# Attention scores of two heads at a time in a float32 two-layer kernel: rotary parts as neighbouring 64-row tiles, mask in fp32r, later turns, output tiles spread

## What is computed

```python
s = (jnp.einsum('bqhd,bkhd->bhqk', qn, k_nope)        # 128 values a head
     + jnp.einsum('bqhr,bkr->bhqk', qr, k_pe)) * sm_scale   # 64 rotary values, key shared by heads
s = jnp.where(q_idx[:, None] >= k_idx[None, :], s, -jnp.inf)
p = jax.nn.softmax(s, axis=-1)
o = jnp.einsum('bhqk,bkhd->bqhd', p, v)
...
y = jnp.concatenate([y_rnn, y_att * silu(ga)], axis=-1) @ w_out
```

## Time and profile before

| what | value |
|---|---|
| runs | 2192.72, 2194.42, 2194.52 us, median 2194.42 |
| profiled execution | 2192.71 us, span 2190.9 us |
| granted TensorE clock, mean | 0.992 |
| TensorE busy | 2144.7 us, 98% |
| VectorE busy | 1282.7 us, 59% |
| ScalarE busy | 780.2 us, 36% |

### The profile page before, as it was taken

The page is one execution under the profiler, slowest core; times in us unless marked ns, Lnnn a source line. Parts: engine busy times, 40 slices in busy tenths (PEclk is TensorE's granted clock), DMA queues, the critical chain, the costliest instruction groups (busy, mean ns, idle before and its releaser), DMA issues.

```text
span 2190.9 us, 27655 instructions
## 1 busy us (share of the span) xinstructions
PE 2144.7 (98%) x9998; PEld 1699.1 (78%) x9998; DVE 1282.7 (59%) x2112; ACT 780.2 (36%) x1023; POOL 88.9 (4%) x130
## 2 busy tenths in 40 slices
PE   7999999999999999999999999989999999999999
PEld 5887877778787778777788888768877778776787
DVE  5567767677777767678752323262237777566333
ACT  5232424323242423334441212352234446554211
POOL 0000000000000000000000000000000001100000
PEclk9999999999999999999999999999999999999999
DMA  6555556555555655555463423433332322012332
GB/s 214 168 152 164 175 153 177 151 146 168 167 164 158 177 151 164 159 156 181 157 226 106 154 96 132 143 103 105 96 88 67 101 75 87 34 58 67 126 115 96
DMA packets 213856, 294.44 MB, mean 134 GB/s; under 512 B 16074, under 2 KB 150114, under 8 KB 212642
## 3 DMA queue, kind: packets, MB, share of 16 engines
q1 hardware_dynamic: 200722, 256.12, 38.1%
q0 software_dynamic: 8624, 29.04, 4.8%
q10 hardware_dynamic: 4448, 8.45, 1.1%
HBM read 273.51 MB, written 20.05 MB: 134 GB/s over the span
## 4 chain that ended last, share of the span: by engine, by line
PE 95%; DVE 2%; ACT 1%; DMA 1%; issue 1%; ACTq 0%; POOL 0%; DVEq 0%; SPq 0%; POOLq 0%
PE ps L2220 28%; PE ps L2221 28%; PE ps L2222 28%; PE ps L2308 2%; PE ps L2312 1%; PE ps L2549 1%; PE ps L2547 1%; PE ps L2569 1%; PE ps L2460 1%; PE ps L2290 1%; PE ps L2550 1%; PE ps L2560 0%; PE ps L2385 0%; PE ps L2292 0%; DMA vrows<-in_kv_a_norm_dram 0%
## 5 line engine op out<-in xcount | busy, mean ns | idle before, releaser
L2220 PE MATMUL ps<-hn_hi,w_hi 128*128 128x512 f32 x1280 | 517.8, 405 | 0.1
L2221 PE MATMUL ps<-hn_lo,w_hi 128*128 128x512 f32 x1280 | 505.6, 395 | 0.0
L2222 PE MATMUL ps<-hn_hi,w_lo 128*128 128x512 f32 x1280 | 505.5, 395 | 0.0
L1658 DVE TENSOR_TENSOR w_lo<-w_raw,w_hi 128x1024 fp32r<-128x1024 f32 x174 | 213.4, 1229 | 426.6 <-ACT w_hi L1047 425.1
L1047 ACT ACTIVATE w_hi<-w_raw 128x1024 fp32r<-128x1024 f32 x174 | 183.8, 1060 | 486.7 <-PE ps L2222 446.3
L1407 DVE TENSOR_TENSOR w_lo<-w_raw,w_hi 128x1024 fp32r<-128x1024 f32 x162 | 198.2, 1224 | 227.7 <-ACT w_hi L920 227.2
L920 ACT ACTIVATE w_hi<-w_raw 128x1024 fp32r<-128x1024 f32 x162 | 171.3, 1058 | 432.3 <-PE ps L2222 413.4
L2220 PEld LDWEIGHTS ps<-hn_hi,w_hi 128*128 128x128 f32 x1280 | 240.1, 188 | 62.6 <-DVE w_lo L1407 3.4
L2221 PEld LDWEIGHTS ps<-hn_lo,w_hi 128*128 128x128 f32 x1280 | 240.2, 188 | 60.7 <-issue 5.0
L2222 PEld LDWEIGHTS ps<-hn_hi,w_lo 128*128 128x128 f32 x1280 | 239.9, 187 | 58.8
L2220 PE MATMUL ps<-w_hi,y_hi 128*128 128x512 f32 x512 | 205.7, 402 | 7.5 <-DVE y_lo L1667 7.5
(11 more groups left out here) (366 smaller groups left out, 2690.3 us busy)
## 6 DMA issues: line engine op xcount, KB each, us to landing
ada_raw<-in_w_ada_dram SPq DMA_DIRECT2D x128, 384.0 KB, 3.4
w_raw<-in_ssm_w_in_dram SPq DMA_DIRECT2D x96, 512.0 KB, 4.6
w_raw<-in_ssm_w_in_dram SPq DMA_DIRECT2D x128, 256.0 KB, 4.2
w_raw<-in_w_in_dram SPq DMA_DIRECT2D x64, 512.0 KB, 3.9
w_raw<-in_ssm_w_out_dram SPq DMA_DIRECT2D x60, 512.0 KB, 3.9
csb<-cs_rows POOLq DMA_DIRECT2D x32, 512.0 KB, 6.8
w_raw<-in_w_out_dram SPq DMA_DIRECT2D x32, 512.0 KB, 3.9
y_rows<-yt POOLq DMA_DIRECT2D x8, 1024.0 KB, 4.7
```

The lines of the kernel that those rows point to most:

```text
L1658: nc.vector.tensor_tensor(w_lo[:, slot, :], w_raw[:, slot, :], w_hi[:, slot, :].bitcast(F32), ALU.subtract).then_inc(lo_ready, 1)
L2220: nc.tensor.matmul(out_, a_hi, b_hi, start=start, stop=False)
L2221: nc.tensor.matmul(out_, a_hi, b_lo, start=False, stop=False)
L2222: return nc.tensor.matmul(out_, a_lo, b_hi, start=False, stop=stop)
```

## The change

A step k is now a query block and a head, `k % 2, k // 2`, so both heads of one block are neighbours. TensorE's `score(p, j)` makes both heads of block j: for each head the 128-row product and the mask, then the two rotary products one behind the other. Identity and mask are copied to fp32r once (`ident_r`, `mask_r`, by ScalarE), and the mask product uses them. The order of TensorE, VectorE and ScalarE within a pair is written anew. Some small buffers move into `ysq`.

```diff
+def head_and_rows(k):
+    return k % 2, k // 2
...
             def turned(g):
...
-                act.wait_ge(root_asked, g + 4)
-                nc.scalar.activation(nrm[:], nrm[:], ACT.Sqrt).then_inc(root_done, 1)
                 act.wait_ge(q_turned, g + 1)
                 for h, bank in enumerate(Q_BANKS):
...
                 if g + 1 < PAIRS:
                     read_tile(g + 1, 0)
+                act.wait_ge(root_asked, g + 4)
+                nc.scalar.activation(nrm[:], nrm[:], ACT.Sqrt).then_inc(root_done, 1)
+                if g + 1 < PAIRS:
                     read_tile(g + 1, 1)
...
                 for k in range(8):
-                    if cur and 1 <= k <= 5:
-                        read_tile(g, k + 2)
+                    if cur and k in (2, 4, 6):
+                        for t in range(k + 1, min(k + 3, 8)):
+                            read_tile(g, t)
+                    if cur and k == 6:
+                        pair_hi(g * 4 + 6)
...
-                        if g + 1 == PAIRS:
-                            make_y2_hi(k - 6)
+                    if g + 1 == PAIRS and k in (4, 5):
+                        make_y2_hi(k - 4)
...
+            act.wait_ge(mask_ready, 1)
+            nc.scalar.activation(ident_r[:], ident[:], ACT.Copy)
+            nc.scalar.activation(mask_r[:], maskn[:], ACT.Copy).then_inc(mask_ready, 1)
             turned(0)
...
+            def score(p, j):
+                if j == 0:
                     pe.wait_ge(qk_ready, 5 * p + 5)
                 behind = 2 if p == PAIRS - 1 else 3
...
+                n = (j + 1) * P
+                at = slice(j * P, n)
+                banks = [score_bank(p, 2 * j + h) for h in range(2)]
+                for h, bank in enumerate(banks):
+                    if 2 * j + h >= behind:
+                        pe.wait_ge(exp_ready, p * 8 + 2 * j + h - behind + 1)
+                    nc.tensor.matmul(ps[:, bank, 0:n], qt[:, h, at], kt[:, h, 0:n], start=True, stop=False)
+                    nc.tensor.matmul(ps[:, bank, j * P:n], ident_r[:], mask_r[:], start=False, stop=False)
+                for h, bank in enumerate(banks):
+                    rows = slice(h * ROPE, (h + 1) * ROPE)
+                    nc.tensor.matmul(ps[:, bank, 0:n], qpt[rows, at], kpt[rows, 0:n], start=False, stop=True
+                                     ).then_inc(scored, 1)
...
-                pe.wait_ge(pt_ready, p * 8 + 4 * h + 4)
+                pe.wait_ge(pt_ready, p * 8 + h + 7)
```

More of the change, by code:

```diff
@@ L331, in build_program @@
         pt = (pt_even, pt_odd)
[L333 removed]
+        prob = [sb(f"prob{i}", [P, (3 + i // 2) * P], F32, scope_a) for i in range(NT)]
+        ident_r = sb("ident_r", [P, P], F32R, scope_a)
+        mask_r = sb("mask_r", [P, P], F32R, scope_a)
         qt = sb("qt", [P, 2, SEQ], F32, scope_a)
@@ L2092, in scores @@
                 cur = g < PAIRS
[L2093 to L2117, removed]
@@ new lines, in scores @@
+                row_max(p, 4)
+                row_max(p, 5)
+                scale_prob(p, 4)
+                keep_prob(p, 2)
+                scale_prob(p, 5)
+                keep_prob(p, 3)
+                if g + 1 == PAIRS:
+                    make_y2_lo(0)
+                    make_y2_lo(1)
+                if not cur:
+                    pair_lo(PAIRS * 4 + 5)
+                    for b in range(10, 14):
+                        make_y2_lo(b)
+                row_max(p, 6)
+                row_max(p, 7)
@@ L2535, in tile @@
                     mm.then_inc(unit_used, 2)
[L2537 to L2542, removed]
+            def score(p, j):
+                if j == 0:
                     pe.wait_ge(qk_ready, 5 * p + 5)
                 behind = 2 if p == PAIRS - 1 else 3
[L2545 to L2551, removed]
+                n = (j + 1) * P
[10 more added lines that the diff above has]
+                                     ).then_inc(scored, 1)
             def turn_prob(p, j):
-                qb = j % 4
+                qb = head_and_rows(j)[1]
                 pe.wait_ge(prob_ready, p * 8 + j + 1)
@@ L2623, in scores @@
                 cur = g < PAIRS
[L2624 to L2632, removed]
+                score(p, 0)
+                if cur:
+                    tile(g, 3)
+                    tile(g, 4)
+                else:
+                    out2_tiles(3)
+                score(p, 1)
+                if cur:
+                    tile(g, 5)
+                else:
+                    out2_tiles(2)
+                turn_prob(p, 0)
+                if not cur:
+                    out2_tiles(1)
+                turn_prob(p, 1)
+                if cur:
+                    tile(g, 6)
+                else:
+                    out2_tiles(1)
+                score(p, 2)
+                turn_prob(p, 2)
+                if not cur:
+                    out2_tiles(1)
+                turn_prob(p, 3)
+                if cur:
+                    tile(g, 7)
+                else:
+                    out2_tiles(1)
+                score(p, 3)
+                turn_prob(p, 4)
+                if not cur:
+                    out2_tiles(1)
                 turn_prob(p, 5)
+                if g + 1 < PAIRS:
+                    tile(g + 1, 0)
+                else:
+                    out2_tiles(1)
                 if cur:
                     turn_q_tok(g)
-                else:
-                    out2_tiles(1)
                 turn_prob(p, 6)
[L2639 to L2643, removed]
+                if not cur:
                     out2_tiles(1)
                 turn_prob(p, 7)
+                if not cur:
+                    out2_tiles(1)
+                head_sum(p, 0)
                 if g + 1 < PAIRS:
                     tile(g + 1, 1)
-                elif cur:
+                else:
                     out2_tiles(1)
```

77 lines of the change are left out of this document (55 added, 22 removed).

## The result

| what | before | after |
|---|---|---|
| median of the compared runs | 2193.57 us (4 runs, 2192.14 to 2194.52) | 2178.64 us (4 runs, 2177.32 to 2181.62) |
| profiled execution | 2192.71 us, span 2190.9 | 2178.15 us, span 2176.6 |
| granted TensorE clock, mean | 0.992 | 0.992 |

The changed kernel is 14.9 us faster, ratio 0.9935 with a 95% interval of 0.9921 to 0.9949. I had forecast 2186.4 with a range of 2182 to 2191: the sign was right, the gain was almost twice the forecast 8.0.

A forecast was written before the change was run, and what follows sets the result against it. TensorE, busy 98% of the span, was taken as the bound. Gains of 4.7 (first two pairs) and 5.5 (third), less 0.4 (entry) and 1.8 (last pair), summed to 8.0 us: forecast 2186.4 us from a 2194.4 median, range 2182 to 2191.

The forecast's parts named there:

- 2.35 + 2.35 + 5.5 - 1.8: Attention pairs, in order: gains forecast for the first, second and third, and a loss of 1.8 us in the last.
- The rotary term, 1.5u: Score block, both heads' 64-row rotary products: half overlapped, taking 1.5u, between bounds of 2u (none) and u (whole).
- u: Streaming time of a float32 matmul of n columns, 4n/2.4 ns at 2.4 GHz: 0.213 us at 128, 0.853 at 512.
- whole overlap: Rival, rotary products: 0.5u less, 1.07 us a pair, only partly in the last pair; 2182 to 2183 us; chance 0.12.
- The mask term, 0.107 + 0.115 each: Score block, each fp32r mask: 0.107 us from the pace of 128-column transposes, plus 0.115 for the float32 to fp32r change.
- 64-row mode, 0.10 + 0.20 a block: Score block, rotary products: 0.10 us to enter 64 rows, 0.20 to leave, once per block rather than twice.
- The walk over the queues: Attention pairs: engine queues followed with estimated durations to find late turns; waits of 0.5, 0.5, 3.3 and 5.5 us.
- turn 7 and head sum 0: First pair, TensorE after the last score: the last probability turn waits 0.15, the first head sum 0.3; 0.5 us lost.
- 3.3 us lost forecast: Third pair: remaining waits at late turns, head sum, head_out and 1.75 at the end for kt and qpt; sum 3.3 us.
- 5.5 us lost forecast: Last pair: waits of 2.3 us at the third output tile and 0.45, 0.9, 1.6, 0.2 at turns; sum 5.5.
- The clock rival: Rival, last pair: clock falls behind the new 2.3 us wait, price 1.6 an event; 2188 to 2190 us; chance 0.17.
- Entry: the 0.4: Before the first pair: ScalarE copies and a tile read delay the square root and hence scale_k; loss 0.4 us.

## Why the prediction was wrong in size

The profiled executions differ by 14.56 us and the sum gave 8.0. The 6.6 between them is 5.7 in the pairs (14.08 against 2.35 + 2.35 + 5.5 - 1.8 = 8.4), 0.56 at and before the entry, and 0.3 outside the span. Two terms of the new score block failed, the rotary parts and the mask.

- **The rotary term, 1.5u, was wrong; it is 1.0u.** I read a float32 product as two instructions that stand in the queue one by one, so that only the middle two of four could pair. The records are two (x2), but the halves take theirs independently, whatever stands between: 2u in place of 3u with each part twice in the order 0, 0, 1, 1. Worth 0.5 x 2.133 = 1.07 a pair. The rival "whole overlap" had the right mechanism, with a chance of 0.12; its 2182 to 2183 still carried the wrong mask term.
- **The mask term, 0.107 + 0.115 each, was wrong; it is 0.09.** The part of 0.107 measured 0.111. The change of type was carried over from a step between a float32 mask and an fp32r tile, where it is still there after the block (0.28 in place of 0.175); between the products it is not. Worth 8 x 0.13 = 1.06 a pair.
- **Both together** are 2.13 a pair: 10.61 forecast less 8.54 measured is 2.07. The first two pairs gained 1.96 more than forecast, the third 2.1. With both corrected in three pairs alone, the sum is 8.0 + 3 x 2.07 = 14.2, against 14.56 measured.
- **64-row mode, 0.10 + 0.20 a block, was right:** the steps of the changed kernel hold it, and a second round a block costs 0.33.
- **The walk over the queues was right.** First pair: TensorE waits 0.34 at head sum 0, which from start to start loses 0.5; turn 7 and head sum 0 were forecast to lose 0.5. Third pair: no wait above 2, and qpt's 1.4 as before; 3.3 us lost forecast, 36.68 - 34.31 = 2.4 idle (2.9 from start to start), and no clock fall. Last pair: 5.5 us lost forecast, 5.5 idle, which from start to start is 6.2.
- **The last pair gave part of the extra gain back,** as the whole-overlap rival said it would. Its length without the clock fall is 41.32, +0.55, where 1.8 less 2.13 would be -0.3. Of these 0.9, 0.7 are the longer waits just named: the turns wait for VectorE, and TensorE that is done sooner waits longer. The kernel with both rotary parts on one half shows the same from the other side: it has 2.13 us more TensorE work in this pair, a clock fall too, and takes 42.88 us against 42.93, with 3.5 idle in place of 5.5.
- **The clock rival came true beside it,** at the price of 1.6 that it named, in the last pair and also at the entry, where I had not looked for it. Its reasoning by the length of the wait did not hold: with the rotary parts apart the clock fell (0.50 from 1985.0 to 1988.4) behind a wait of 1.41, and it stayed up in three traces behind 2.46.
- **Entry: the 0.4 was right, and so was its reason.** VectorE stands idle 0.41 to 0.42 for the root in all ten traces with this entry, and not in the trace of before; TensorE's wait grew from 1.9 to between 2.2 and 2.4. What came on top, the clock fall of 1.6 behind it, was not in the sum.
- **The rest, ahead of the stage.** It began 2.2 us earlier than in the trace of before, and lost 2.0 of that at the entry. Most of the head start comes from the 25 us from 1020 on, where the trace of before was granted a mean clock of 0.93 and the changed kernel's 1.00: 0.07 x 25 = 1.75 us. The change doesn't touch that stretch, and in the second trace of the changed kernel its mean clock is 0.93 too. So this part of the trace's gain comes and goes between executions.

## What to carry to other kernels

Two products with 64 rows of contraction each, on different halves of TensorE's array and in different PSUM banks, cost as much as one (both in one bank was not tried); put them next to each other, and share the 0.3 us of going into 64 rows and back. Order work in queues so that such neighbours can stand, and don't expect the order itself to pay: here the order alone gave a ratio of 1.0003. Where a faster TensorE block makes VectorE the one that is waited for, read each turn's wait and move what VectorE does ahead of it; here that gave another 4.5 us. Before such a move, follow what stands behind the place that the work moves to: at the entry two copies moved ahead of the tile reads cost what the earlier root gave.

## What the runs showed of the chip

- Float32 products on the two halves of the array overlapped whole (four records of 512 columns in 1.06 us), also when queued 0, 0, 1, 1 (1.93 us for eight records, against 1.91 for four on one half).
- A 128-column fp32r matmul between float32 ones cost 0.09, one more behind it 0.111, a float32 one 0.22.
- Of eight traces in which TensorE waited 2.2 to 2.5 us at an output tile of the last pair, five show the granted clock down behind it (0.96 over the pair) and the pair 1.6 us longer, and three don't. The kernels with each rotary part twice differ in nothing else there: 44.25 and 42.64. At the entry it is the same: behind waits of 2.2 to 2.4 us the clock fell in five traces of twelve. What decides it was not found.
